# A two-layer hybrid decoder trunk on one core: attention's half swap by transfers, and other places for blocks and weights at the seams

## The reference, cut to what matters

```python
def reference(x, positions, ...):
    cos, sin = rope_tables(positions, DIFF_HD)
    for i in range(2):
        m = gated_deltanet(x, ...) if i == 0 else diff_attention(x, cos, sin, ...)
        x = layer_norm(DEEPNORM_ALPHA * x + m, ln_mix_g[i], ln_mix_b[i])
        f = conv_ffn(x, ffn_w_up[i], ffn_conv_w[i], ffn_conv_b[i], ffn_w_down[i])
        x = layer_norm(DEEPNORM_ALPHA * x + f, ln_ffn_g[i], ln_ffn_b[i])
    return x

def diff_attention(x, cos, sin, w_in, ..., subln_w, w_out, lambda_init):
    q, k, v = jnp.split(x @ w_in, 3, axis=-1)        # 8 heads of 2 halves of 64
    q, k = apply_rope(q, cos, sin), apply_rope(k, cos, sin)
    # per head: two causal softmax maps of scores q k / 8
    # p = softmax(s0) - lam * softmax(s1);  o = p @ v
    o = rms_norm(o, subln_w) * (1.0 - lambda_init)
    return o.reshape(B, T, D_MODEL) @ w_out

def apply_rope(x, cos, sin):
    x1, x2 = jnp.split(x, 2, -1)                     # halves of 32
    return jnp.concatenate([x1 * cos - x2 * sin, x2 * cos + x1 * sin], -1)
```

## Time and profile before

| | us |
|---|---|
| median of 3 runs | 1441.07 |
| lowest, highest | 1439.88, 1441.41 |
| profiled execution, time | 1440.98 |
| profiled execution, span | 1439.2 |
| mean granted PE clock | 0.994 of 2.4 GHz |

### The profile page before, as it was taken

The page is one execution under the profiler, slowest core; times in us unless marked ns, Lnnn a source line. Parts: engine busy times, 40 slices in busy tenths (PEclk is TensorE's granted clock), DMA queues, the critical chain, the costliest instruction groups (busy, mean ns, idle before and its releaser), DMA issues.

```text
span 1439.2 us, 20166 instructions
## 1 busy us (share of the span) xinstructions
PE 1398.7 (97%) x7042; PEld 1141.6 (79%) x7042; DVE 868.1 (60%) x1361; ACT 649.8 (45%) x1042; POOL 79.8 (6%) x92
## 2 busy tenths in 40 slices
PE   8799999999999999999999999999999999999997
PEld 7688888788788888888887876667688888888886
DVE  4566776666666666666524637777686666665226
ACT  4665666666433444444312235665524444443211
POOL 3000000000000000000001111111000000000002
PEclk9999999999999999999999999999999999999999
DMA  6122111121112333334322132121222333334331
GB/s 189 54 67 66 45 51 50 51 66 59 60 44 60 111 93 100 91 100 137 123 96 95 59 88 60 43 74 58 74 74 73 103 88 102 94 105 140 100 102 60
DMA packets 157727, 118.84 MB, mean 83 GB/s; under 512 B 5899, under 2 KB 145645, under 8 KB 157677
## 3 DMA queue, kind: packets, MB, share of 16 engines
q1 hardware_dynamic: 157676, 118.17, 27.4%
HBM read 116.04 MB, written 2.11 MB: 82 GB/s over the span
## 4 chain that ended last, share of the span: by engine, by line
PE 87%; DVE 8%; ACT 2%; issue 1%; DMA 1%; POOL 0%; SPq 0%; DVEq 0%; ACTq 0%
PE bank L1613 16%; PE bank L1615 16%; PE bank L1614 16%; PE bank L1601 8%; PE bank L1603 8%; PE bank L1602 8%; PE bank L1672 3%; PE bank L1679 2%; PE bank L1987 1%; PE bank L2005 1%; PE bank L1670 1%; PE bank L1948 1%; DVE w_lo L361 1%; PE bank L1579 1%; DVE Tc L1137 1%
## 5 line engine op out<-in xcount | busy, mean ns | idle before, releaser
L1613 PE MATMUL bank<-x_hi,w_hi 128*128 128x512 f32 (+1 forms) x1160 | 459.8, 396 | 3.6 <-DVE x_lo L1026 2.6
L1615 PE MATMUL bank<-x_hi,w_lo 128*128 128x512 f32 (+1 forms) x1160 | 438.3, 378 | 0.0
L1614 PE MATMUL bank<-x_lo,w_hi 128*128 128x512 f32 (+1 forms) x1160 | 437.7, 377 | 0.0
L361 DVE TENSOR_TENSOR w_lo<-raw,w_hi 128x1024 fp32r<-128x1024 f32 x194 | 237.9, 1229 | 243.8 <-ACT w_hi L356 238.4
L356 ACT ACTIVATE w_hi<-raw 128x1024 fp32r<-128x1024 f32 x186 | 195.0, 1051 | 168.9 <-PE bank L1603 139.6
L1613 PEld LDWEIGHTS bank<-x_hi,w_hi 128*128 128x128 f32 x1160 | 219.6, 189 | 42.0 <-issue 4.2
L1615 PEld LDWEIGHTS bank<-x_hi,w_lo 128*128 128x128 f32 x1160 | 218.9, 189 | 41.1
L1614 PEld LDWEIGHTS bank<-x_lo,w_hi 128*128 128x128 f32 x1160 | 219.7, 189 | 36.1 <-issue 2.9
L1601 PE MATMUL bank<-w_hi,u_hi 128*128 128x512 f32 x416 | 164.8, 396 | 3.0 <-DVE w_lo L361 3.0
L1603 PE MATMUL bank<-w_hi,u_lo 128*128 128x512 f32 x416 | 162.5, 391 | 0.0
L1602 PE MATMUL bank<-w_lo,u_hi 128*128 128x512 f32 x416 | 162.4, 390 | 0.0
(11 more groups left out here) (292 smaller groups left out, 1787.3 us busy)
## 6 DMA issues: line engine op xcount, KB each, us to landing
raw<-in_ffn_w_up SPq DMA_DIRECT2D x88, 512.0 KB, 3.8
raw<-in_ffn_w_down SPq DMA_DIRECT2D x44, 512.0 KB, 3.2
raw<-in_gdn_w_in SPq DMA_DIRECT2D x32, 512.0 KB, 4.1
raw<-in_diff_w_in SPq DMA_DIRECT2D x24, 512.0 KB, 3.7
raw<-in_gdn_w_out SPq DMA_DIRECT2D x8, 512.0 KB, 3.4
raw<-in_diff_w_out SPq DMA_DIRECT2D x8, 512.0 KB, 3.3
x_tok<-in_x SPq DMA_DIRECT2D x4, 512.0 KB, 5.9
ROW<-decay_rows SPq DMA_DIRECT2D x8, 256.0 KB, 3.1
```

Source lines behind the costliest of these rows:

```text
L361: nc.vector.tensor_tensor(w_lo[:, s, :], raw[:, (base + r) % RAW, :], w_hi[:, s, :].bitcast(F32), ALU.subtract).then_inc(lo_ready, 1)
L1613: nc.tensor.matmul(out, hi, x_hi[:, k, cols], start=(k == 0), stop=False)
L1614: nc.tensor.matmul(out, hi, x_lo[:, k, cols], start=False, stop=False)
L1615: ins = nc.tensor.matmul(out, lo, x_hi[:, k, cols], start=False, stop=last)
```

## The change

1. The half swap is no longer a product. After its copy to `qk_raw`, `take` on ACT issues four transfers, each of 32 partitions (64 KB), from `qk_raw` into a new tile `qk_rot` with neighbouring groups of 32 exchanged. DVE's `rope` waits for these and multiplies by a column of signs `turn_sign` (made once by a reduction of `swap`) and by sin in one instruction. `rotate` is gone from PE.
2. The projections run `AHEAD = 4` units ahead: in head h, `fill(a, b)` issues units a+4 to b+4 of head h+1, and past 16 the first units of head h+2. The units that stood ahead of the scores now stand behind them. In the last two heads the places are filled by a new `ATT_FILL`, with four pieces in the last four places of head 6.
3. On DVE the k rotation moves from the start of a head to the end of the one before, behind the clamp. On ACT `take` of k moves ahead of the weight's high half and of the P copy of block 3. The weights held for the output projection are split one place earlier, chunk 2 at the end of head 6. The loops run two rounds; heads 5, 6 and 7 are written out.
4. GDN's last head: DVE's low half of chunk 7 moves ahead of kk and L, KD ahead of the held low half, and ACT's held high halves move one copy later.
5. `ffn_start`: block 2 is turned ahead of the fourth early tile. `down` of layer 0: block 0 is turned one unit later, block 1 behind the first of V's units.

```diff
-ATT_FILL = [(0, 0, 0, 0), (1, 0, 0, 1), (2, 0, 1, 0), (3, 0, 1, 1), (5, 0, 0, 2), (6, 0, 1, 2), (7, 0, 0, 3),
+ATT_FILL = [(-4, 0, 0, 0), (-3, 0, 0, 1), (-2, 0, 1, 0), (-1, 0, 1, 1), (1, 0, 0, 2), (2, 0, 1, 2), (5, 0, 0, 3),
+            (6, 0, 1, 3), (8, 0, 0, 4), (8, 0, 1, 4), (9, 1, 0, 0), (9, 1, 1, 0), (10, 1, 0, 1), (10, 1, 1, 1),
...
+AHEAD = 4
...
@@ ACT, GDN step @@
                 if more:
                     split_hi(act, C_GDN_IN, h, 8)
-                else:
-                    hold_hi(act, C_GDN_OUT + WS + 1, (o_dve, O_N * h))
                 copied(LEVELS[1])
...
-                    hold_hi(act, C_GDN_OUT + WS + 2, (o_dve, O_N * h))
+                    hold_hi(act, C_GDN_OUT + WS + 1, (o_dve, O_N * h))
                 copied(LEVELS[2])
@@ ACT, attention @@
             def take(g, kind):
...
+                    act.wait_ge(rot_loaded[kind], 64 * g)
                 nc.scalar.activation(qk_raw[kind][:, :], bank[kind][:, :], ACT.Copy,
                                      scale=(HD ** -0.5 if kind == 0 else 1.0)).then_inc(bank_read[kind], 1)
+                wait_read(act, kind, T_QK // 2 + g)
+                act.wait_ge(rope_head, R_DVE0 - RD_N + RD_N * g + RD["rope2 " + "qk"[kind]])
+                for b in range(4):
+                    to, src = b * P // 4, (b ^ 1) * P // 4
+                    nc.scalar.dma_start(qk_rot[kind][to:to + P // 4, :],
+                                        qk_raw[kind][src:src + P // 4, :]).then_inc(rot_loaded[kind], 16)
...
                 exps(3)
                 turned_p(2)
                 if more:
+                    take(h + 1, 1)
                     split_hi(act, C_QK, it, 2 * r + 5)
...
                 turned_p(3)
+                if isinstance(h, int) and h == HEADS - 2:
+                    split_hi(act, C_QK, it, 2 * r + 6)
...
-                if more:
-                    take(h + 1, 1)
@@ DVE, GDN step @@
                 if not more:
                     gated(h - 1, 1 - e)
+                    split_lo(dve, C_GDN_IN, h, 7)
                 pe("kk")
...
-                if not more:
-                    split_lo(dve, C_GDN_IN, h, 7)
                 solve(h, e)
...
                 masked(0)
+                nc.vector.tensor_tensor(KD[e][:, :, :], v3(X(e, 2)), bc(kdecs), ALU.mult).then_inc(d_dve, 1)
                 if not more:
                     hold_lo(dve, C_GDN_OUT + 4)
-                nc.vector.tensor_tensor(KD[e][:, :, :], v3(X(e, 2)), bc(kdecs), ALU.mult).then_inc(d_dve, 1)
@@ DVE, attention @@
+            nc.vector.tensor_reduce(turn_sign[:, :], swap[:, :], AX.X, ALU.add, negate=True).then_inc(lam_dve, 1)
...
-                dve.wait_ge(rot_pe, 2 * g + kind + 1)
-                nc.vector.tensor_tensor(rope2[kind][:, :], bank[4 + kind][:, :], sin[:, :], ALU.mult).then_inc(rope_head, 1)
+                dve.wait_ge(rot_loaded[kind], 64 * g + 64)
+                nc.vector.scalar_tensor_tensor(rope2[kind][:, :], qk_rot[kind][:, :], turn_sign[:, 0:1], sin[:, :],
+                                               ALU.mult, ALU.mult).then_inc(rope_head, 1)
...
-                rope(h, 1)
+                maxima(0)
                 if not first:
                     row_factor(h - 1)
-                maxima(0)
-                if not first:
                     scaled_out(h - 1)
...
                 mix(1)
-                maxima(2)
-                split_lo(dve, C_QK, it, 2 * r + 4)
                 if not more:
                     split_lo(dve, C_QK, it, 2 * r + 5)
+                maxima(2)
+                if more:
+                    split_lo(dve, C_QK, it, 2 * r + 4)
+                else:
+                    hold_lo(dve, C_ATT_OUT + 4)
...
                 nc.vector.tensor_scalar(att_o[:, :], bank[3][:, :], ROOT_MAX, -ROOT_MAX, ALU.min,
                                         ALU.max).then_inc(n_dve, 1)
+                if more:
+                    rope(h + 1, 1)
+                if isinstance(h, int) and h == HEADS - 2:
+                    split_lo(dve, C_QK, it, 2 * r + 6)
@@ PE @@
                 up_tile(l, 2, early)
+                turn_out(2 * l, 2)
                 up_tile(l, 3, early)
-                turn_out(2 * l, 2)
                 turn_out(2 * l, 3)
...
-                    if l == 0 and tb == NT - 1:
-                        turn_out(1, 0)
...
-                        if l == 0 and tb == NT - 1 and k == JT - 1:
-                            turn_out(1, 1)
+                        if l == 0 and tb == NT - 1 and k == JT - HELD + 1:
+                            turn_out(1, 0)
                         down_unit(l, tb, k)
...
+            v_unit(0, 0)
+            turn_out(1, 1)
+            v_unit(0, 1)
...
                 def fill(p0, p1):
+                    u0, u1 = p0 + AHEAD, p1 + AHEAD
+                    if not last:
+                        project_qk(h + 1, (r + 1) % 2, u0, min(u1, 2 * KT))
+                        if not (isinstance(h, int) and h == HEADS - 2):
+                            project_qk(h + 2, r % 2, max(u0 - 2 * KT, 0), u1 - 2 * KT)
...
-                fill(0, 1)
-                rotate(h, 1)
-                fill(1, 3)
                 pe.wait_ge(rope_head, R_DVE0 + RD_N * h + RD["kr"])
                 scores(0)
                 scores(1)
-                fill(3, 4)
+                fill(0, 4)
...
-                if not last:
-                    rotate(h + 1, 0)
                 turn(3)
```

More of the change, by code:

```diff
@@ L245, in build @@
         rope2 = [place("uh", 4 + i, f"rope2{i}", [P, T]) for i in range(2)]
+        qk_rot = [place("uh", 7 + 3 * i, f"qk_rot{i}", [P, T]) for i in range(2)]
         qr = place("uh", 6, "qr", [P, T])
@@ L767, in step @@
                 else:
+                    hold_hi(act, C_GDN_OUT + WS + 2, (o_dve, O_N * h))
+                copied(LEVELS[3])
+                if not more:
                     hold_hi(act, C_GDN_OUT + WS + 3, (o_dve, O_N * h))
-                copied(LEVELS[3])
                 if more:
@@ L999, in _ @@
             step(0, 0)
-            with act.Fori(0, PAIRS - 1) as it:
+            with act.Fori(0, PAIRS - 2) as it:
                 for r in (1, 2):
                     step(it, r)
-            step(0, HEADS - 1)
+            for h in range(HEADS - 3, HEADS):
+                step(0, h)
             out_hi(HEADS - 1)
@@ L1556, in _ @@
             rope(0, 0)
+            rope(0, 1)
             split_lo(dve, C_QK, 0, 3)
             step(0, 0)
-            with dve.Fori(0, PAIRS - 1) as it:
+            with dve.Fori(0, PAIRS - 2) as it:
                 for r in (1, 2):
                     step(it, r)
-            step(0, HEADS - 1)
+            for h in range(HEADS - 3, HEADS):
+                step(0, h)
             row_factor(HEADS - 1)
@@ L1922, in v_unit @@
                 unit(1, tb, k, C_V + k, KT, x_hi, x_lo, tb == NT - 1, k == KT - 1)
-            for tb, k in itertools.product(BOTH, BOTH):
-                v_unit(tb, k)
+            v_unit(0, 0)
+            turn_out(1, 1)
+            v_unit(0, 1)
+            v_unit(1, 0)
+            v_unit(1, 1)
             turn_out(1, 2)
@@ L1943, in project_qk @@
                     block_products(kind, (C_QK + 2 * odd + kind) % WS, k, k == KT - 1)
-            def rotate(g, kind):
-                wait_read(pe, kind, T_QK // 2 + g)
-                nc.tensor.matmul(bank[4 + kind][:, :], swap[:, :], qk_raw[kind][:, :], start=True,
-                                 stop=True).then_inc(rot_pe, 1)
             def turned_out(h):
@@ L1970, in fill @@
                 def fill(p0, p1):
-                    if last:
-                        for tb, half, k in [piece for p, *piece in ATT_FILL if p0 <= p < p1]:
+                    u0, u1 = p0 + AHEAD, p1 + AHEAD
[3 more added lines that the diff above has]
+                            project_qk(h + 2, r % 2, max(u0 - 2 * KT, 0), u1 - 2 * KT)
+                    shift = 0 if last else 2 * KT
+                    if isinstance(h, int) and h >= HEADS - 2:
+                        for tb, half, k in [piece for p, *piece in ATT_FILL if p0 <= p + shift < p1]:
                             if (tb, k) == (0, 0):
@@ L2044, in _ @@
             project_qk(0, 0, 0, 2 * KT)
+            project_qk(1, 1, 0, AHEAD)
             pe.wait_ge(v_out, 2 * NT)
-            rotate(0, 0)
             step(0, 0)
-            with pe.Fori(0, PAIRS - 1) as it:
+            with pe.Fori(0, PAIRS - 2) as it:
                 for r in (1, 2):
                     step(it, r)
-            step(0, HEADS - 1)
+            for h in range(HEADS - 3, HEADS):
+                step(0, h)
             pe.wait_ge(t_act, 1 + (HEADS - 1) * TA_N + TA["exp", 3, 1])
```

31 lines of the change are left out of this document (16 added, 15 removed), and 5 rows, old and new, of the table ATT_FILL.

## The result

| | us | ratio to before, 95% interval |
|---|---|---|
| kernel before, 4 runs beside it | 1441.24 (1439.88 to 1444.42) | |
| changed kernel, 4 runs | 1476.01 (1474.02 to 1478.70) | 1.0232 [1.0214, 1.0251] |
| profiled execution, span | 1472.3, where it was 1439.2 | |

Forecast was 1446.5, range 1435.8 to 1451.5. The sign is right, the size wrong by 29.5 us.

The account below looks back on a forecast made before the run. PE, busy 97% of the span, was taken to bound the kernel. Attention +6.5 us and seams -0.95 gave +5.55 on the profiled 1440.98: 1446.5, range 1435.8 to 1451.5.

Parts of the forecast that it names:

- I take 0.33, the row nearest in kind: Heads' tail on ACT: each of four transfer issues costs 0.33 us, holding ACT to 2.95; bounds nothing and 0.43.
- Rival (a): ACT's issues cost next to nothing, a head changes by -0.48 us, and the whole takes 1435.2, faster; chance 0.24.
- Each 0.1 us of an issue is 0.4 a head: ACT's queue between k's copy and the weight's high half: 0.1 us per issue costs 0.4 a head, 3.2 in all.
- nothing, at worst 0.5 a head: ACT's issues for q, 1.3 us ahead of exps(3), cost nothing, at worst 0.5 a head.
- Rival (b): New waits in each head lower the clock, each fall costing about 1.3 us: 9 more, 1455.6; chance 0.10.
- The term of -0.3: First head: copy, issues, landing of 2.1 and two operations take 5.5 us for 5.8 before; with landing 3.7, +1.3.
- Rival (c): The swap lands late behind a weight load; at 6 us landing, 7 x 1.4 more, 1456; chance 0.04.
- Forecast +1.4 and nothing: Ahead of the last head, waiting 2.8 us for the low half costs +1.4; last head nothing, between -4 and +2.
- Forecast -0.95: Seams together: GDN's last head +0.85 us, down projection to V -1.2, both ffn_start -0.6.
- GDN's +0.85: GDN's last head: L starts 2.4 us later, the chain ends 1.95 later, partly regained; net +0.85, down to -1.5.
- remove the 1.6 for POOL: Down projection to V: turning blocks 0 and 1 later removes PE's 1.6 us wait for POOL; net -1.2.
- Removing the swaps was worth 2.0 a head: Attention heads: taking the half swaps off PE is worth about 2.0 us a head, some 16 in all.

Follow-up runs that it names:

- sp_ahead5: Changed kernel with SP issuing, projections five units ahead, ACT's high half and k copy before block 2's P copy, DVE's k rotation before the clamp: 1437.85 us, ratio 0.9965.
- k_by_sp: Changed kernel with k's four transfers issued by SP and q's four by ACT: 1460.19 us, ratio 1.0126 to the kernel before.
- sp_issues: Changed kernel with SP instead of ACT issuing all eight transfers of a head, between its two weight loads: 1449.96 us, ratio 1.0045 to the kernel before.

## Why the prediction was wrong, step by step

**The term that failed: the price of an issue.** The step "I take 0.33, the row nearest in kind" took the four small stores of SP; the bounds were nothing and 0.43. Measured 0.51 for the first and 0.61 for the others, 2.44 for four with the gaps, where I had 1.3. No row of ACT existed, and two rows of another queue with other shapes were taken for a ceiling. The trace of the kernel before had dearer ones in that same queue, small loads ahead of attention:

```profile
656.13 0.71 SPq L424 DMA_DIRECT2D lamv<-in_diff_lam_q  x1
```

Rival (a) lay on the other side, and no case had an issue dearer than 0.43. At 0.61 the prediction's own slope (3.2 us for each 0.1) gives 1455.5, so the price alone is 9 of the 29.5 us; the rest is what follows.

**The sensitivity.** "Each 0.1 us of an issue is 0.4 a head": k's four give 1.1 more that way, but the tail grew by 2.46 (F to the scores 11.13 for the forecast 8.67) and the head by 2.51. The rest by link: the copy of k ended 2.26 behind F, not 1.6, since q's issues had held the exponentials of block 3 (+0.7). I had written "nothing, at worst 0.5 a head" for q's issues, since DVE had ended Pm(3) 0.6 ahead of where PE would want it. Four issues hold exps(3) for 2.4, far more than that slack. My reason beside it, that exps(3) had waited for maxima, was a misreading too. In the kernel before they stood in ACT's queue right behind the copy of q, which had waited for its bank:

```profile
912.46 0.60 ACT L936 ACTIVATE qk_raw<-bank 128x512 f32<-128x512 f32 x1 [1.04 <-PE bank L1615]
912.95 0.68 ACT L948 ACTIVATE Eb<-bank,att_col 128x512 f32<-128x512 f32 x1
```

On DVE q's sum took 0.96 in place of 0.69 (+0.3) beside POOL's copy. Together 1.1 + 0.7 + 0.3 are 2.1 of the 2.5. Of the other 0.4, about 0.2 are the gaps on ACT on either side of the issues (929.03 to 929.14, 931.58 to 931.70), and the rest steps of 0.1 and less between DVE's rows.

**The clock.** Rival (b) had 0.10 and 1.3 each. It happened: the waits became 1.4 for P and 2.7 for kr, not 0.7 and 2.4, and about every second round fell, 1.7 each. By the idle products 6.5 us in five rounds of the traces, 7 by the runs' ratios.

**Landing.** Right from the second head on: 2.0 for k, and kr never waited for it. In the first head it did: k's four were issued right behind a weight load, landed in 2.7 to 3.8, and DVE stood 2.3 for them. The term of -0.3 with its 2.1 of landing failed there; the stretch grew by 1.4, near the +1.3 that I gave for a landing of 3.7. Rival (c) was not the cause of the rest; for q beside a weight load the landing was 2.5 to 3.4 in the head shown and mattered only once its rotation was moved ahead.

**The round into the last head, and the last head.** Forecast +1.4 and nothing. The round into the last head took 26.5, 1.9 over a steady one, with the wait for w_lo (3.5 where I had 2.8) and a fall of the clock; the last head cost 1.2, within its bounds.

**Seams.** Forecast -0.95, runs -2.3 (-3.7 to -0.7), with GDN's +0.85 met in the trace (+0.9). What failed in the sum is "remove the 1.6 for POOL": a wait of 1.0 for it stayed in the kernel with the seams alone, since block 0 still stands ahead of its norm's end. Of the 1.8 forecast for the down projection and ffn_start its trace shows 0.5, and the runs' gain is mostly the granted clock's, not the sum's.

**Removing the swaps was worth 2.0 a head, as I read.** What the prediction had right is that this gain is given back as a wait for kr. With SP issuing the exchange is 2.0 for 2.0, and 21.24 for 21.28.

## What to carry to other kernels

- A transfer costs its issuing engine time in order, here per issue and not per byte (0.61 us for 64 KB, 0.63 for 32 KB). On an engine that also computes, count it as an instruction of 0.6 us until a row says otherwise, and look for whoever is queued behind it, on that engine and on the next. An engine with nothing urgent should issue.
- Where work is taken from the bounding engine, ask what its wait will be for; here a gain came only when the chain that replaces it was shortened too, by one unit more ahead and the copy first.
- For an operation with no row, look at every row of the queue, the dear ones too, and let the upper bound lie well above the nearest. A small price in a serial tail is multiplied: twice a head, seven times, and then by the clock.

## What the runs showed of the hardware

- An issue of a transfer between two tiles on chip, 32 partitions by 2 KB: 0.51 us for the first of a row and 0.61 for the others on ACT, 0.51 and 0.59 on SP, against 0.33 to 0.58 for SP's 512 KB weight loads in attention. Half the bytes, 0.63. In the changed kernel most land in 1.9 to 2.1 us alone and in 2.4 to 3.8 beside a weight load. The Trainium skill ("DMA: Bandwidth & Descriptors", section "Issuing engines are not separate DMA queues") calls the sequencer time saved by spreading issues "usually small relative to the DMA itself"; here four issues take 2.4 us and one landing 2.0, and moving the eight of a head to SP was worth 27 us in all.
- An instruction of DVE with two inputs in SBUF that starts beside POOL's product of 128x512 ends a fixed time after POOL's has ended, a little less than its own length: the low half 1.08 us after (it took 1.54 and 2.31 in place of 1.22), q's rotation 0.55 after (1.53 in place of 0.74). In `sp_ahead5` POOL ends at 937.33 and DVE's 2.31 end at 938.42. Before the change the rotation read a bank of PSUM and sin, and beside the same POOL product it took 0.69 (922.90, POOL from 921.85 to 923.13): reading `qk_rot` from SBUF exposed it. This agrees with the Trainium skill ("SBUF — State Buffer", section "🔬 SBUF: two separate sides"), by which the pair of ports that the two share is locked for a whole instruction, on DVE's side where two inputs lie in SBUF. Here that decides what moving an instruction of DVE by a microsecond is worth.
- PE's waits of 1.4 and 2.7 us in one head were followed by 3.4 us at 1.2 GHz in about every second head, and idle products in them kept 2.4 GHz in five heads in a row: 6.5 us gained there by doing more. In `k_by_sp` one wait of 2.2 a head was enough for a fall in every round; in `sp_issues` two of four rounds with a wait of 2.0 fell.
